# Rotation tables made once, ahead of the layers, and the first norm's root ahead of the first high parts

## What is computed

```python
h = rms_norm(x, attn_norm_g[l]); proj = h @ w_in[l]
rq, rk, rv, rg, dq, dk, dv = split(proj)            # 512 columns each
ret = rms_norm(retention_bidir(rq, rk / 8, rv, -exp(decay_f), -exp(decay_b))) * silu(rg)
da  = rms_norm(diff_attention(rms_norm(dq), rms_norm(dk), dv, lam, slopes)) * (1 - lam_init)
x = x + concat(ret, da) @ w_out[l]
h = rms_norm(x, ffn_norm_g[l]); x = x + (silu(h @ w_gate[l]) * (h @ w_up[l])) @ w_down[l]
```

```python
inv = 10000.0 ** (-arange(16) / 16); ang = positions[..., None] * inv
cos, sin = cos(ang), sin(ang)
rotated = concat(x1 * cos - x2 * sin, x2 * cos + x1 * sin)
```

## Time and profile before

| | us |
|---|---|
| median of 3 runs (2469.9 to 2478.68) | 2473.1 |
| the profiled execution | 2474.66 |
| its span, first to last instruction | 2472.8 |
| PE busy | 2006.3 (81%) |
| DVE busy | 1613.9 (65%) |
| POOL busy | 1283.9 (52%) |
| ACT busy | 656.8 (27%) |
| chain that ended last | DMA 37%, PE 35%, DVE 16% |

### The profile page before, as it was taken

How to read it: one execution, slowest core, us unless ns; L and a number is a source line. 1 busy time by engine, 2 the same in 40 slices (tenths; PEclk the granted TensorE clock), 3 DMA queues, 4 the chain that set the end, 5 groups by cost and what they waited for, 6 DMA issues and landing times.

```text
span 2472.8 us, 25831 instructions
## 1 busy us (share of the span) xinstructions
PE 2006.3 (81%) x8464; PEld 1317.3 (53%) x8464; DVE 1613.9 (65%) x3725; ACT 656.8 (27%) x1186; POOL 1283.9 (52%) x840
## 2 busy tenths in 40 slices
PE   7889998788998866898777777787768987777776
PEld 6668997668998754454332233266634442223232
DVE  8743116853113668887878887557598887888765
ACT  4344443344443622111011111045321211010100
POOL 6627885637886035655545444230365654444441
PEclk9879999889999878999999999997889999999999
DMA  4405553415555227999999999851299999999995
GB/s 167 137 27 166 191 187 128 134 50 165 198 180 213 84 94 298 421 415 422 420 422 421 422 422 421 359 195 60 86 396 420 416 416 422 421 421 421 421 421 248
DMA packets 117996, 700.21 MB, mean 283 GB/s; under 512 B 13952, under 2 KB 13952, under 8 KB 51840
## 3 DMA queue, kind: packets, MB, share of 16 engines
q0 software_dynamic: 73728, 536.90, 52.3%
q1 hardware_dynamic: 44160, 161.96, 19.3%
HBM read 697.76 MB, written 1.05 MB: 283 GB/s over the span
## 4 chain that ended last, share of the span: by engine, by line
DMA 37%; PE 35%; DVE 16%; issue 5%; POOL 3%; ACT 3%; SPq 0%; DVEq 0%; POOLq 0%; ACTq 0%
PE ps L598 34%; DMA late_row<-in_table,arena 22%; DMA arena<-in_table,arena 12%; DMA row_sb<-in_table,arena 3%; DVE late_row L2042 2%; POOL w_split L1054 2%; DVE arena L1602 1%; DVE arena L2042 1%; DVE diag L2052 1%; POOL arena L1147 1%; DVE arena L1785 1%; DVE arena L1599 1%; ACT w_split L1187 1%; PE ps L630 1%; DVE trig L1494 1%
## 5 line engine op out<-in xcount | busy, mean ns | idle before, releaser
L1054 POOL TENSOR_TENSOR w_split<-raw,w_split 128x1024 fp32r<-128x1024 f32 x260 | 634.0, 2463 | 395.7 <-ACT w_split L1187 392.4
L598 PE MATMUL ps<-late_row,diag 128*128 128x512 f32 x1000 | 480.6, 626 | 130.1 <-DVE diag L2052 130.1
L598 PE MATMUL ps<-arena,diag 128*128 128x512 f32 x888 | 432.5, 631 | 146.5 <-DVE diag L2052 146.1
L598 PE MATMUL ps<-hT_hi,w_split 128*128 128x256 f32 x2624 | 503.6, 290 | 11.7 <-POOL w_split L1054 5.5
L1147 POOL DMA_INDIRECT late_row<-in_table,arena x250 | 305.5, 1222 | 304.6 <-PE ps L598 279.8
L598 PEld LDWEIGHTS ps<-hT_hi,w_split 128*128 128x128 f32 x2624 | 419.8, 193 | 23.2 <-issue 9.2
L598 PEld LDWEIGHTS ps<-late_row,diag 128*128 128x128 f32 x1000 | 189.0, 197 | 410.9 <-DVE diag L2052 214.1
L1147 POOL DMA_INDIRECT arena<-in_table,arena x222 | 256.6, 1156 | 280.0 <-PE ps L598 251.1
L2042 DVE CUSTOM_DVE_ANT_0 late_row<-late_row,x_res 128x1024 f32<-128x1024 f32 x250 | 318.3, 1277 | 121.1 <-DMA late_row<-in_table,arena 120.7
L598 PEld LDWEIGHTS ps<-arena,diag 128*128 128x128 f32 x888 | 168.3, 199 | 393.1 <-DVE diag L2052 221.6
L598 PE MATMUL ps<-hT_lo,w_split 128*128 128x256 f32 x1312 | 374.4, 285 | 0.0
(11 more groups left out here) (235 smaller groups left out, 1951.8 us busy)
## 6 DMA issues: line engine op xcount, KB each, us to landing
raw<-in_stream SPq DMA_DIRECT2D x288, 512.0 KB, 3.3
row_sb<-in_row SPq DMA_DIRECT2D x2, 2306.5 KB, 10.9
late_row<-in_table,arena POOLq DMA_INDIRECT x250, 24.9
arena<-in_table,arena POOLq DMA_INDIRECT x222, 24.0
arena<-in_sub SPq DMA_DIRECT2D x2, 1024.0 KB, 11.4
arena<-in_small SPq DMA_DIRECT2D x2, 640.0 KB, 8.5
x_res<-in_x SPq DMA_DIRECT2D x1, 1024.0 KB, 4.9
out_x<-x_res SPq DMA_DIRECT2D x1, 1024.0 KB, 4.0
```

Source lines behind the costliest of these rows:

```text
L598: ins = nc.tensor.matmul(o, lhsT, rhs, start=start, stop=stop)
L1054: pool.tensor_tensor(w_lo[pair], raw[:, at % raws, :], w_hi[pair].bitcast(F32), ALU.subtract).then_inc(lo_ready, 1)
```

## The change

1. `angles` is called once, behind the constants and ahead of the layer loops. It works on both tiles, and for most steps on sine and cosine together: 13 instructions of 2 to 64 columns in place of 35 in each layer.
2. ScalarE takes both sines ahead of its layer loops, and GpSimd waits for them (`trig_ready`) in `rotate`.
3. SyncE issues positions and frequencies ahead of x and the first chunks.
4. In a layer of block 1 ScalarE takes the first norm's root ahead of the high parts of chunks 0 and 1.

```diff
@@ SyncE
-            sp.dma_start(x_res[:], x_in.rearrange("(t p) d -> p t d", p=P)).then_inc(x_loaded, 16)
-            load_early(0)
             with nc.allow_non_contiguous_dma(reason="256 positions"):
                 sp.dma_start(pos_i, pos_in.rearrange("(t p) -> p t", p=P)).then_inc(setup_in, 16)
             sp.dma_start(invf, inv_in.partition_broadcast(P)).then_inc(setup_in, 16)
+            sp.dma_start(x_res[:], x_in.rearrange("(t p) d -> p t d", p=P)).then_inc(x_loaded, 16)
+            load_early(0)
@@ GpSimd, rotate
                 after_emptied(pool, banks2, "krT")
+                pool.wait_ge(trig_ready, 2)
@@ ScalarE, block1
+                root(1, std_x, ss_x, 1.0 / D, eps1)
                 w.upto(0)
-                root(1, std_x, ss_x, 1.0 / D, eps1)
                 act.wait_ge(par_ready, 32)
...
-                act.wait_ge(turn_ready, 1)
-                A(sin_t[:], turns[:, 0], ACT.Sin)
-                A(cos_t[:], turns[:, 1], ACT.Sin)
                 act.wait_ge(out_full, 1)
@@ ScalarE, ahead of the layers
             act.wait_ge(const_ready, CONSTS)
+            act.wait_ge(angles_ready, 1)
+            A(sin_t[:], turns[:, 0], ACT.Sin).then_inc(trig_ready, 1)
+            A(cos_t[:], turns[:, 1], ACT.Sin).then_inc(trig_ready, 1)
@@ VectorE, angles
                 for t in range(TT):
-                    step(V.tensor_scalar(angle, invf, pos_f[:, t:t + 1], None, ALU.mult))
-                    step.settle()
-                    for b in range(2):
-                        r, n = turns[:, b, t, :], turn_n[:, b, t, :]
-                        step(V.tensor_scalar(n, angle, float(1 / two_pi), 0.25 * b, ALU.mult, ALU.add))
...
+                    step(V.tensor_scalar(angle[:, t, :], invf, pos_f[:, t:t + 1], None, ALU.mult))
+                step.settle()
+                for b in range(2):
+                    step(V.tensor_scalar(turn_n[:, b], angle, float(1 / two_pi), 0.25 * b, ALU.mult, ALU.add))
+                step.settle()
+                step(V.tensor_scalar(turn_n, turn_n, big, None, ALU.add))
+                step.settle()
+                step(V.tensor_scalar(turn_n, turn_n, -big, None, ALU.add))
+                step.settle()
+                both = angle.unsqueeze(1).broadcast_to([P, 2, TT, 16])
+                for k, c in enumerate(parts):
+                    step(V.scalar_tensor_tensor(out=turns, in0=turn_n, scalar=-c, in1=both if k == 0 else turns,
+                                                op0=ALU.mult, op1=ALU.add))
+                    step.settle()
...
@@ VectorE, block1
                 dve.sem_inc(dist_ready, 1)
-                angles(step)
@@ VectorE, ahead of the layers
             setup()
+            angles()
```

More of the change, by code:

```diff
@@ L182, in two_blocks_kernel @@
         sin_t = sb("sin_t", [P, TT, 16])
[L183 to L186, removed]
+        trig = sb("trig", [P, 180])
+        invf, pos_f, pos_i = trig[:, 0:16], trig[:, 16:18], trig[:, 18:20].bitcast(I32)
+        angle = trig[:, 20:52].rearrange("p (t f) -> p t f", t=TT)
+        turns = trig[:, 52:116].rearrange("p (b t f) -> p b t f", b=2, t=TT)
+        turn_n = trig[:, 116:180].rearrange("p (b t f) -> p b t f", b=2, t=TT)
         eps1 = sb("eps1", [P, 1])
@@ L374, in two_blocks_kernel @@
         const_ready = sem("const_ready")
+        angles_ready = sem("angles_ready")
+        trig_ready = sem("trig_ready")
         x_loaded = sem("x_loaded")
@@ L379, in two_blocks_kernel @@
         dist_step = sem("dist_step")
+        angle_step = sem("angle_step")
         opened = sem("opened")
@@ L396, in two_blocks_kernel @@
         emptied = dict(act=sem("act_emptied"), dve=sem("dve_emptied"))
-        turn_ready = sem("turn_ready")
         dve_step = sem("dve_step")
@@ L1470, in setup, with angles @@
                     step(V.tensor_scalar(alibi[:, h], absd[:], -(2.0 ** (-2.0 * (h + 1))), None, ALU.mult))
-            def angles(step):
+            def angles():
+                step = Steps(dve, angle_step)
                 dve.wait_ge(setup_in, 32)
@@ L1482, in angles @@
                 for t in range(TT):
-                    step(V.tensor_scalar(angle, invf, pos_f[:, t:t + 1], None, ALU.mult))
-                    step.settle()
-                    for b in range(2):
-                        r, n = turns[:, b, t, :], turn_n[:, b, t, :]
-                        step(V.tensor_scalar(n, angle, float(1 / two_pi), 0.25 * b, ALU.mult, ALU.add))
-                        step.settle()
-                        step(V.tensor_scalar(n, n, big, None, ALU.add))
-                        step.settle()
-                        step(V.tensor_scalar(n, n, -big, None, ALU.add))
-                        step.settle()
-                        for k, c in enumerate(parts):
-                            step(V.scalar_tensor_tensor(out=r, in0=n, scalar=-c, in1=angle if k == 0 else r,
-                                                        op0=ALU.mult, op1=ALU.add))
-                            step.settle()
-                        step(V.tensor_scalar(r, r, float(np.pi / 2) * b, PI, ALU.add, ALU.min))
-                        step.settle()
-                        step(V.tensor_scalar(r, r, -PI, None, ALU.max))
-                        step.settle()
@@ L1501, in angles @@
-                dve.sem_inc(turn_ready, 1)
+                    step(V.tensor_scalar(angle[:, t, :], invf, pos_f[:, t:t + 1], None, ALU.mult))
[6 more added lines that the diff above has]
+                step(V.tensor_scalar(turn_n, turn_n, -big, None, ALU.add))
@@ new lines, in angles @@
+                step.settle()
[3 more added lines that the diff above has]
+                                                op0=ALU.mult, op1=ALU.add))
+                    step.settle()
+                for b in range(2):
+                    step(V.tensor_scalar(turns[:, b], turns[:, b], float(np.pi / 2) * b, PI, ALU.add, ALU.min))
@@ L1503, in _ @@
+                step.settle()
+                step(V.tensor_scalar(turns, turns, -PI, None, ALU.max))
+                step.settle()
+                dve.sem_inc(angles_ready, 1)
             class Transposed:
```

## The result

The changed kernel takes 2438.37 us, median of 4 runs (2437.88 to 2449.37); the kernel before, run beside it, 2473.28 (2469.9 to 2478.68). The ratio is 0.9876, 95% interval 0.9854 to 0.9899: faster by 25 to 36 us. The forecast was 2447.4, range 2440 to 2459: the median lies 1.6 us under the range, and the interval of the ratio (2437 to 2448) reaches into it.

What follows compares the result with a forecast made beforehand. The bound taken was TensorE's wait in both layers of block 1 for VectorE's dq copy, late behind angles slowed by GpSimd. Gains of 11.8 and 13.9 us, together 25.7, gave 2447.4 us from a median of 2473.1; range 2440 to 2459.

Steps and rivals of the forecast that it cites:

- The stall at rv: TensorE's wait at rv for VectorE's dq0 copy, and slow matmuls behind, go: 11.3 us in layer 1, 10.4 in layer 2.
- then each takes 2.3 us: Layer 1 angles: the first 18 of 35 instructions take 0.21 us each, those after 2.3 us each beside GpSimd's low parts.
- (a): GpSimd's eleven low parts, chunks 10 to 20, could be late, squares holding them up 2.6 us in all; taken as 0.
- (b): Sums of squares of dq and dk, needed by ScalarE's root at 80.8, end at 76.2, in time.
- The start of layer 1: TensorE starts at 11.5; hT_lo comes 0.8 us later, less the 1.38 us wait at the decay's exponential: 0.5 us won.
- the rival of late positions: Positions land after 6.9 us even in front, so the first norm starts 3.7 us later: 2451; chance 0.15.
- the drain: Start of layer 1: ScalarE waits 1.28 us after each of two table loads, starting 2.6 us later: 2450; chance 0.02.
- The start of layer 2: hT_lo 0.8 us earlier, held by lines 1587 and 1588; ScalarE's 2.7 us wait at the decay's exponential goes: 3.5 us.
- The sum: Both layers of block 1: 11.8 us in layer 1 and 13.9 in layer 2, together 25.7 us.
- The full gain at the starts: Layer starts: VectorE isn't held by low parts 0 and 1, 5.4 us more gained: 2442; chance 0.12.
- The stall didn't move: Rival: all twelve operations on dq and dk wait like line 1630, so TensorE stalls at dv: 2470; chance 0.06.
- The clock didn't fall in the projections: Rival: 1.2 GHz granted in rv, dv and rg without the pause, 33 us more a layer: 2513; chance 0.02.

Runs made afterwards that it cites:

- e1: The changed kernel run again with no edit; median 2440.41 us (4 runs), ratio to before 0.9849 to 0.9896.
- e4: Kernel before, with 13 wider angle instructions in place of 35, still inside both layers at the old place; 2445.17 us, ratio 0.9860 to 0.9914.
- e5: Kernel before, all 35 angle instructions kept but with operands in PSUM, at most one in SBUF each; 2444.17 us, ratio 0.9848 to 0.9918.
- e6: Kernel before, with the 35 angle instructions done twice in each layer; 2490.18 us, ratio 1.0054 to 1.0120.
- e8: The change, with SyncE's loads in the old order, x and three chunks ahead of positions and frequencies; 2446.06 us (1 run), no interval.
- e12: The changed kernel a third time, no edit; 2438.14 us (1 run), no interval.
- e11: The kernel before run again, no edit; 2474.60 us (1 run), no interval.
- e2: The change, with the first norm's root put back behind the first two high parts; 2450.02 us, ratio to before 0.9871 to 0.9926.
- e3: Kernel before, with only the first norm's root moved ahead of the first two high parts; 2477.15 us (10 runs), ratio 0.9997 to 1.0043.
- e7: The change, with the small products of parameters and ScalarE's exponential of lambda moved behind the decays; 2442.46 us, ratio to before 0.9844 to 0.9902.

## Why the prediction was right

**The stall at rv (11.3 and 10.4 us): right, with one reading too wide.** It is gone in both layers, and so are the slow matmuls behind it: in layer 1 TensorE is busy for 27.00 of 27 us at a granted clock of 1.00, as the window of the change's dq, dk and rv shows (columns as in e1):

```profile
52.00:79.00 27.00, 27.00 (x121) 22.36 (x120) 12.67 (x12) 10.86 (x12) 26.01 (x11) 1.00 0.60 213
```

e4, e5 and e6 test the reason from three sides: fewer instructions, the same in PSUM, twice as many. In e5 only operands moved, and S came 9.5 and 10.5 us earlier; nearly all that is missing of the 11.3 is the clock behind TensorE's wait at the third dq chunk. The prediction's "then each takes 2.3 us" holds for eleven instructions and not for the last six (e6), but its sum used the 31 us and the waits as the rows have them. The Trainium skill (SBUF — State Buffer, SBUF: two separate sides) has GpSimd and those VectorE instructions that run in a two-port mode, or have two inputs in SBUF, take a shared pair of ports as a lock for a whole instruction. The trace agrees, with 2.3 us for 16 columns beside low parts of 2.35 us; the ports themselves no run here shows.

**What is late next: right in size.** (a) The low parts: squares at 1.75 to 2.0 us each in layer 1 lengthened the run of eleven by 1.9 us (2.6 was the bound), and in 52:79 TensorE waits for none of them. But the low parts are close: GpSimd's share of the chain has grown by four points. (b) The sums of squares ended at 72.7, and I had 76.2: copies and reductions ran at 0.64 to 0.69 as assumed, and squares below the 2.8 taken from line 1630.

**The start of layer 1 (0.5 won): right in sum, by luck in two terms.** Angles ended at 6.92 (7.0), TensorE began at 11.53 (11.5), `hT_lo` at 17.21 (17.6 said, 16.79 before). The two small loads and x, issues of SyncE in 0:60 of the change (KB, median us to landing):

```profile
x_res<-in_x SPq DMA_DIRECT2D x1, 1024.0 KB, 5.7
...
trig<-in_pos SPq DMA_DIRECT2D x1, 1.0 KB, 2.1
trig<-in_inv SPq DMA_DIRECT2D x1, 8.0 KB, 3.0
```

They landed in 2.1 and 3.0 us, between my bounds 1.7 and 6.9 and near the one I took, so the rival of late positions fell; e8 shows what it would have cost. But x took 5.7 us to land (4.9 before) and so held the norm to 7.72, not 7.0. On the other side the 0.6 us by which the table loads were to reach past VectorE's sums was nothing: they ended at 10.00, and the root waited for the sums until 10.19. The two misses cancel in 11.53. TensorE went on at its third dq chunk at 50.64 and not 51.35, 0.7 us won. The table loads of the two sines and the root took 1.28 us each; the first sine began 0.01 us behind its load (8.35), and the root 0.19 us behind its own, held by VectorE. So the drain had no part in it, against the Trainium skill (ScalarE: Activation LUTs, What ACT_TABLE_LOAD costs).

**The start of layer 2 (3.5 won): 2.4 measured, and the reason named wrongly.** `hT_lo` began 9.5 us behind the sums, before 10.8: 1.4 won and not 0.8. It was held not by lines 1587 and 1588 (0.18 and 0.27 us, now 1593 and 1594) but by line 1585's two dots, which I had left out of the argument, 2.2 to 2.4 us each; the two one-column sums waited 1.7 to 2.3 each behind it, which I had not seen either. Of the 2.69 us of ScalarE's wait, which the prediction had go whole, 0.98 stayed, and the exponential and TensorE's third dq chunk came 2.4 us earlier, counted from the sums. Together layer 2 won 12.7 us, and 13.9 was said. That e1 and e12 won 14.4 is the clock: TensorE waits 2.2 to 2.3 us at that chunk in both profiles of the change, but behind the wait the first had 0.58 granted in 426:429 and e1 had 1.00 in the same stretch of its layer.

**The sum: 25.7 said.** By S the two profiles of before and the three of the change differ by 26.5 on average (224.8 against 198.3 for the two layers, 24.7 to 27.9 by pair). The measurements by time are larger: 34.9 by the medians of the result (25 to 36 by its interval), 30.7 in e1, 36.5 between e11 and e12. So by S the sum is right within 1 us, and by time it is too small: some 4 to 10 us stand in none of its terms, and I can't assign them. They are why the median fell under the range. Candidates are the granted clock behind S, 11 to 13 us a layer, which was at 1.2 GHz in one of four layers of before and one of six of the change, and block 2, which varied between 1695 and 1703 us in runs of the same code. Neither is shown to differ between the kernels. One thing on record speaks for the clock: the mean granted clock of an execution goes with its time. The five longest of 36 executions of before (2482.11 to 2485.29) had 0.926 to 0.931, the six shortest (2461.17 to 2466.99) 0.934 to 0.938, and the nine of the change 0.938 to 0.943. But a part of that is the slow stretch behind the stall, which the sum has, and e11 had a mean of 0.928 although both its stretches behind S were at the upper level. So this stays open.

**The other rivals.** The full gain at the starts (2442) is nearest by time, but the trace speaks against it: VectorE is held for 4.5 us between scaling and `hT_lo`. The stall didn't move: copies under GpSimd took 0.69. The clock didn't fall in the projections. What the prediction did not weigh is that the clock could differ behind S, in a stretch that the change doesn't touch.

**What each part is worth.** Fewer instructions in place give 9 and 10.6 us of S (e4). The tables ahead of the layers and the early loads without the root give 6.9 and 10.7 (e2): by S no more than e4, so to leave the layers won nothing here beside making the instructions fewer. The root's move gives 7 to 9 on top of the tables, part of it by the clock, and 3.6 alone (e3), where the copy still comes at the end of GpSimd's run: S1 and S2 sum to 224.0, 220.4, 206.5 and 197.7 to 199.3 in before, e3, e2 and the change.

## What to carry to other kernels

Where a chain of tiny VectorE instructions from SBUF to SBUF runs beside a long run of GpSimd, cost each at a whole GpSimd instruction for as long as that run lasts: here eleven instructions of 16 columns took 25.85 us. Give them an operand in PSUM (e5), or merge them so that they fit into a pause of GpSimd (e4); each of these alone took the stall away. To move them out of the loop was tried only with the merged ones (e2).

Check what fills the place that they leave. A wait of 3 to 4 us of TensorE further on, at the third dq chunk, cost about 1.5 us more than its length, in lower clock, and shortening the work ahead of it (e7) won nothing where it closed GpSimd's pause.

## What the runs showed of the hardware

- A VectorE instruction on one column took 1.74 and 2.30 us, a dot of 64 columns 2.23 to 2.38, and a square of 512 columns 1.75 to 2.4 while GpSimd subtracted (means of each pair, both layers), against 0.16, 0.23 and 0.64 in the pauses of e7 and e6 (lines 1607, 1600, 1616). With a PSUM operand, 16 columns took 0.17 to 0.24 in e5 throughout. The other way round, a low part that met a square took 2.83 to 2.86 us and not 2.4.
- Behind a wait of TensorE of 3.0 us (e5) and 4.0 us (e2, e4) at the third dq chunk of layer 1, the granted clock fell to 0.50, 0.66 and 0.60 in 53:56; behind waits of 1.3 us (the change) and 2.7 us (before) it stayed at 1.00 there. In layer 2 of the change it fell behind 2.3 us (0.58 in 426:429), and in e1 it did not behind 2.2.
- One program showed either level of TensorE's clock after the same work. The first profile of the change, two windows around S:

```profile
98.00:103.00 5.00, 4.57 (x24) 3.10 (x22) 1.31 (x2) 3.43 (x4) 5.00 (x3) 1.00 0.54 167
103.00:106.00 3.00, 2.52 (x14) 2.07 (x15) 1.41 (x5) 0.00 (x0) 3.00 (x3) 0.94 0.74 261
```

and e1:

```profile
98.00:103.00 5.00, 4.56 (x24) 3.10 (x22) 1.31 (x3) 3.43 (x4) 5.00 (x3) 1.00 0.50 167
103.00:106.00 3.00, 2.53 (x16) 2.08 (x17) 1.41 (x5) 0.00 (x0) 3.00 (x3) 1.00 0.73 257
```

TensorE was busy for the same time in both up to the point where the grant fell in one of them, and then stayed at 0.50 although the engine was busy for 7.00 of 7 us (108:115). What decides it stays open; no edit here was made to control it.
- A pause of GpSimd of 2.9 us in layer 2 (3.9 in layer 1) made eight decay instructions 8.7 us shorter (2.72 against 11.45 in layer 2 of e7).
